# Opening each stage on centred instead of normed tiles at eight layer norms, a new order inside all norms, and the head norms of the second mixer among projections and chunks

## What is computed

```python
# first block, 2 layers: y is an RWKV-7 mixer (layer 0), a gated delta net (layer 1)
    u = x * (1 + sc1) + sh1
    y = mixer(u)
    x = _layer_norm(DEEPNORM_ALPHA * x + (1 + ga1) * y, ln_g[i, 0], ln_b[i, 0])
    u = x * (1 + sc2) + sh2
    gate, up = jnp.split(u @ ffn_w_in[i], 2, axis=-1)
    y = (jax.nn.silu(gate) * up) @ ffn_w_out[i]
    x = _layer_norm(DEEPNORM_ALPHA * x + (1 + ga2) * y, ln_g[i, 1], ln_b[i, 1])
# the delta net's head norms: q and k before the chunks, o behind them
    q = _l2norm(q) * d ** -0.5;  k = _l2norm(k)
    o = _rms_norm(o, norm_g, 1e-6) * jax.nn.silu(z)
# second block, 2 layers: SSD, FoX and MLA branches side by side between two SwiGLU stages
    h = layer_norm(ALPHA * h + 0.5 * swiglu(h, gate1, up1, down1), ln1_g, ln1_b)
    h = layer_norm(ALPHA * h + mix, ln2_g, ln2_b)
    h = layer_norm(ALPHA * h + 0.5 * swiglu(h, gate2, up2, down2), ln3_g, ln3_b)
```

## Time and profile before

| | |
|---|---|
| profiled execution | 2309.86 us, span 2308.0 us |
| median of three executions | 2300.97 us |
| mean granted clock of TensorE | 0.954 |
| TensorE busy | 2120.9 us, 17730 matmuls |
| VectorE busy | 1211.5 us |
| ScalarE busy | 869.0 us |
| GpSimd busy | 707.0 us |
| idle time of TensorE before high-by-high matmuls, put down mostly to ScalarE's normed tile | 63.6 us, 38.0 of them |
| weight splits on GpSimd | 105, 4.67 us each |
| weight splits on VectorE | 132, 2.42 us each |

### The profile page before, as it was taken

How to read it: one execution, slowest core, us unless ns; L and a number is a source line. 1 busy time by engine, 2 the same in 40 slices (tenths; PEclk the granted TensorE clock), 3 DMA queues, 4 the chain that set the end, 5 groups by cost and what they waited for, 6 DMA issues and landing times.

```text
span 2308.0 us, 40812 instructions
## 1 busy us (share of the span) xinstructions
PE 2120.9 (92%) x17730; PEld 1923.8 (83%) x17730; DVE 1211.5 (52%) x2208; ACT 869.0 (38%) x1258; POOL 707.0 (31%) x316
## 2 busy tenths in 40 slices
PE   3989997999889988999999889899999998988997
PEld 3867875889889887898999885699989997857897
DVE  6156444764582446653642656554265428457652
ACT  0442111444353223543433443343343334434543
POOL 0340001314674003126314550131461165304124
PEclk9998998999999989999999998899999999989999
DMA  8564442455434003554445340244434543303552
GB/s 327 226 270 148 149 149 74 146 183 186 157 132 147 2 2 128 186 196 166 162 168 183 128 147 19 91 165 167 181 134 176 175 173 110 128 19 146 184 191 83
DMA packets 49682, 340.44 MB, mean 148 GB/s; under 512 B 6368, under 2 KB 8416, under 8 KB 8672
## 3 DMA queue, kind: packets, MB, share of 16 engines
q1 hardware_dynamic: 49504, 337.84, 40.5%
HBM read 336.77 MB, written 1.05 MB: 146 GB/s over the span
## 4 chain that ended last, share of the span: by engine, by line
PE 80%; DVE 12%; ACT 3%; issue 2%; DMA 2%; POOL 1%; SPq 0%; ACTq 0%; POOLq 0%; DVEq 0%
PE bank L532 80%; DMA ada_ring<-ada 2%; POOL ring_low L2516 1%; DVE arena L1899 1%; DVE arena L1884 1%; ACT high L1471 1%; DVE small L1894 1%; PE bank L538 1%; DVE arena L1927 1%; DVE arena_parts L1922 1%; DVE arena L1914 0%; DVE ZZ L2108 0%; DVE arena L2096 0%; DVE small L2482 0%; DVE small L2371 0%
## 5 line engine op out<-in xcount | busy, mean ns | idle before, releaser
L532 PE MATMUL bank<-arena_parts,high 128*128 128x272 f32 (+2 forms) x4512 | 1028.0, 315 | 63.6 <-ACT arena_parts L1496 38.0
L532 PEld LDWEIGHTS bank<-arena_parts,high 128*128 128x128 f32 x4512 | 751.6, 192 | 114.0 <-issue 52.1
L532 PE MATMUL bank<-arena_parts,ring_low 128*128 128x272 f32 (+2 forms) x2736 | 782.9, 289 | 0.0
L1471 ACT ACTIVATE high<-ring 128x2048 fp32r<-128x2048 f32 x237 | 453.1, 1914 | 681.0 <-PE bank L532 597.1
L2516 POOL TENSOR_TENSOR ring_low<-ring,high 128x2048 fp32r<-128x2048 f32 x105 | 489.7, 4666 | 690.4 <-ACT high L1471 690.3
L532 PEld LDWEIGHTS bank<-arena_parts,ring_low 128*128 128x128 f32 (+1 forms) x2736 | 524.3, 192 | 0.9
L1935 DVE TENSOR_TENSOR ring_low<-ring,high 128x2048 fp32r<-128x2048 f32 x132 | 318.7, 2415 | 185.6 <-ACT high L1471 185.6
L532 PE MATMUL bank<-hidden_high,high 128*128 128x256 f32 (+1 forms) x1056 | 303.2, 287 | 0.0
L532 PE MATMUL bank<-hidden_low,high 128*128 128x256 f32 (+1 forms) x1056 | 301.1, 285 | 0.0
L532 PE MATMUL bank<-hidden_high,ring_low 128*128 128x256 f32 (+1 forms) x1056 | 300.1, 284 | 0.0
L2516 POOL TENSOR_TENSOR hidden_low<-arena,hidden_high 128x256 fp32r<-128x256 f32 (+1 forms) x132 | 105.6, 802 | 586.1 <-DVE hidden_high L1951 585.9
(11 more groups left out here) (330 smaller groups left out, 2272.5 us busy)
## 6 DMA issues: line engine op xcount, KB each, us to landing
ring<-stream SPq DMA_DIRECT2D x269, 1024.0 KB, 4.8
ada_ring<-ada SPq DMA_DIRECT2D x48, 1024.0 KB, 5.6
con<-consts SPq DMA_DIRECT2D x1, 1542.5 KB, 11.5
con<-consts SPq DMA_DIRECT2D x1, 1040.0 KB, 7.1
arena<-xin SPq DMA_DIRECT2D x1, 1024.0 KB, 11.8
out<-arena SPq DMA_DIRECT2D x2, 512.0 KB, 2.9
prob_even<-consts SPq DMA_DIRECT2D x1, 320.0 KB, 11.8
par<-params SPq DMA_DIRECT2D x1, 272.5 KB, 9.7
```

What stands on the lines that cost most here:

```text
L532: ins = nc.tensor.matmul(o, l, r, start=start, stop=stop_, skip_group_check=True)
L1471: act(high[:, q % HIGHS], ring[:, s % RING], ACT.Copy).then_inc(a.sig(high_ready), 1)
```

## The change

1. **Raw openings.** At eight norms (all but 3 and 9) the next stage's first four output tiles are no longer computed from normed tiles but from the centred tiles times the gain, which exist before the variance is known. These raw tiles are split as well: ScalarE writes the high part (`raw_tile`), VectorE the low part (`raw_rest`). Each raw tile carries four further columns with the gain and the bias (high and low), so that the same matmuls, now 260 or 276 columns wide, give the weights' products with gain and bias. `raw_four` issues these matmuls in another order (the eight high ones of a tile, then the four low ones), with the norm's own mean matmuls inside the first tile.
2. **Scaling afterwards.** When the reciprocal of the deviation is there, VectorE mends each of the four banks (`scale_opened`: a reduction of the four columns, one or two multiply-adds, one multiplication). The bias goes into the Silu of the gate, into the product with the up tile, or is added in the bank.
3. **New order in every norm, 3 and 9 too.** All centrings stand behind the variance (three behind the reciprocal), the split of slab 2 moves from GpSimd to VectorE in front of the first normed tile, and ScalarE writes both the high part and the whole input. GpSimd no longer splits between the normed tiles; in a mixer stage slab 3 is split there by GpSimd once the last low part is made.
4. **Base tiles later.** `residual_base` leaves the norm: in a feed-forward stage with a raw opening it stands behind f=1, in mixers behind the third convolution.
5. **A shift for the last tile.** `early_mean` gains a third matmul, half_mean into bank 6, from which the last tile's centring reads.
6. **Head norms of the delta net.** The sums and spreadings of q and k move among the last eight projection tiles. The squares of the output are made per chunk by ScalarE and summed by TensorE inside the chunk loop (`output_sums`), with one small result per group of four heads.

The core of the diff:

```diff
 def low_by_vector_engine(q):
 
     n = max(i for i in range(len(STAGES)) if STAGE_AT[i] <= q)
-    return STAGES[n] == "ffn" and HIGHS <= q - STAGE_AT[n] < HIGHS + FT
+    at = q - STAGE_AT[n]
+    return at == HIGHS - 1 or STAGES[n] == "ffn" and HIGHS <= at < HIGHS + FT
...
                 eng.wait_ge(*freed(4))
                 mm(bank[4][:, 0:T], cm("mean"), x_sums(0, T), True, False)
                 mm(bank[4][:, 0:T], cm("mean"), x_sums(1, T), False, False)
+                mm(bank[6][:, 0:T], cm("half_mean"), x_sums(0, T), True, True, hold=True).then_inc(full["vector"][6], 1)
...
+            def raw_four(n, tiles, T, signals):
+
+                for b in range(4):
+                    eng.wait_ge(*freed(b))
+                eng.wait_ge(square_added, pe.nth(square_added, 6))
+                eng.wait_ge(raw_high_ready, pe.nth(raw_high_ready, 1))
+                eng.wait_ge(raw_low_ready, pe.nth(raw_low_ready, 1))
+                for k in range(DT):
+                    eng.wait_ge(raw_high_ready, pe.nth(raw_high_ready))
+                    eng.wait_ge(raw_low_ready, pe.nth(raw_low_ready))
+                    blocks = [split_block((*tile, k)) for tile in tiles]
+                    both, low = raw_both(n, k, T), raw_low(n, k, T)
+                    if k == DT - 1:
+                        for b, (w_high, w_low) in enumerate(blocks):
+                            m = mm(bank[b][:, 0:T], w_high, low, False, False, hold=b == 3)
+                        m.then_inc(opened, 1)
+                    for b, (w_high, w_low) in enumerate(blocks):
+                        if k == 0 and b == 2:
+                            mean_sum(T)
+                        mm(bank[b][:, 0:T + 4], w_high, both, k == 0, False)
+                        m = mm(bank[b][:, 0:T + 4], w_low, both, False, k == DT - 1, hold=k == DT - 1)
+                        if k == DT - 1:
+                            m.then_inc(signals[b], 1)
+                    if k == 0:
+                        square_sum(T)
+                    if k < DT - 1:
+                        for b, (w_high, w_low) in enumerate(blocks):
+                            m = mm(bank[b][:, 0:T], w_high, low, False, False, hold=b == 3)
+                        m.then_inc(opened, 1)
+
+            def normal_tile():
+
+                eng.wait_ge(input_high_ready, pe.nth(input_high_ready))
+                eng.wait_ge(input_low, pe.nth(input_low))
+
...
-            left(-(-at[0] // BLOCKS))
-
+            project_by_parts("gdn", "gdn_in", 0, 2, SEQ, [0, 1], "scalar", n0=24)
             eng.wait_ge(a2p, pe.nth(a2p))
             token_sums(8, 4)
             token_sums(3, 5)
+            project_by_parts("gdn", "gdn_in", 0, 2, SEQ, [2, 3], "scalar", n0=26)
             eng.wait_ge(v2p, pe.nth(v2p))
-            spread_scale(0, B4)
+            spread_scale(0, [4, 5, 6, 7])
+            project_by_parts("gdn", "gdn_in", 0, 2, SEQ, [0, 1], "scalar", n0=28)
             eng.wait_ge(v2p, pe.nth(v2p))
-            spread_scale(1, B4)
+            spread_scale(1, [4, 5, 6, 7])
+            project_by_parts("gdn", "gdn_in", 0, 2, SEQ, [2, 3], "scalar", n0=30)
+            left(-(-at[0] // BLOCKS))
 
             eng.wait_ge(a2p, pe.nth(a2p))
...
+            def output_sums(p, c):
+
+                eng.wait_ge(head_squares, pe.nth(head_squares, 2))
+                if c == 0:
+                    eng.wait_ge(*freed(3))
+                for hb in range(4):
+                    m = mm(bank[3][:, 2 * hb + c:2 * hb + c + 1], tl(US, 4 * p + hb, SEQ, META)[:, P * c:P * c + P], one[:, :],
+                           True, True, hold=c and hb == 3)
+                if c:
+                    m.then_inc(closing(3, "vector"), 1)
...
+            def raw_tile(n, j, T):
+                act(raw_high(n, j, T), tl(9, j, T), ACT.Copy, scale=lnc[:, n, 0, j:j + 1]).then_inc(a.sig(raw_high_ready), 1)
...
+            def norm_out(n, T):
+                raw = n in OPENED_RAW
+                weights_high(STAGE_AT[n] + 2)
+                if raw:
+                    done = a.nth(opened, DT) - DT
                 for j in range(DT):
                     eng.wait_ge(normed, a.nth(normed))
-                    if n < len(STAGES):
-                        act(input_high(STAGES[n], j, T), tl(9, j, T), ACT.Identity, bias=lnc[:, n, 1, j:j + 1],
+                    if raw:
+                        eng.wait_ge(opened, done + max(min(j + 2, DT - 1), j + 1))
+                    for to, signal in ((input_high(STAGES[n], j, T), input_high_ready), (tl(US, j, T, xview(T)), whole_ready)):
+                        act(to, tl(9, j, T), ACT.Identity, bias=lnc[:, n, 1, j:j + 1],
                             scale=lnc[:, n, 0, j:j + 1]).then_inc(a.sig(signal), 1)
...
+            def raw_rest(n, js, T):
...
+                for j in js:
+                    if j == 0:
+                        eng.wait_ge(raw_high_ready, v.nth(raw_high_ready))
+                        for i, (to, gains, part) in enumerate(raw_columns(n, T, 1)):
+                            nv.tensor_tensor(to, gains, part.bitcast(F32), ALU.subtract).then_inc(v.sig(raw_low_ready if i else vstep), 1)
+                    eng.wait_ge(raw_high_ready, v.nth(raw_high_ready))
+                    nv.scalar_tensor_tensor(out=raw_low(n, j, T), in0=tl(9, j, T), scalar=lnc[:, n, 0, j:j + 1],
+                                            in1=raw_high(n, j, T).bitcast(F32), op0=ALU.mult,
+                                            op1=ALU.subtract).then_inc(v.sig(raw_low_ready), 1)
...
+            def norm(n, T, order):
+                raw = n in OPENED_RAW
+                raw_rest(n, order[1][0], T)
                 eng.wait_ge(full_for_vector[4], v.nth(full_for_vector[4]))
-                nv.tensor_tensor(small[:, 0, 0:T], bank[4][:, 0:T], small[:, 1, 0:T], ALU.subtract).then_inc(v.sig(shift_ready), 1)
-
+                nv.tensor_tensor(small[:, 0, 0:T], small[:, 1, 0:T], bank[4][:, 0:T], ALU.subtract).then_inc(v.sig(shift_ready), 1)
+                raw_rest(n, order[1][1], T)
+                eng.wait_ge(full_for_vector[5], v.nth(full_for_vector[5]))
+                eng.wait_ge(shift_squared, v.nth(shift_squared))
+                nv.scalar_tensor_tensor(out=small[:, 1, 0:T], in0=bank[5][:, 0:T], scalar=EPS_LN, in1=small[:, 2, 0:T],
+                                        op0=ALU.add, op1=ALU.subtract).then_inc(v.sig(var_ready), 1)
+                raw_rest(n, order[1][2], T)
...
                 centers = [center(0)]
-                eng.wait_ge(full_for_vector[5], v.nth(full_for_vector[5]))
...
                 nv.reciprocal(small[:, 2, 0:T], small[:, 1, 0:T]).then_inc(v.sig(vstep), 1)
+                centers += [center(1), center(2), center(3)]
+                if n < len(STAGES):
+                    weights_low(STAGE_AT[n] + 2)
+
+                def normed_pair(q):
+                    for j in (2 * q, 2 * q + 1):
+                        eng.wait_ge(*centers[3])
+                        nv.tensor_tensor(tl(9, j, T), tl(XAS, j, T, xview(T)), small[:, 2, 0:T], ALU.mult).then_inc(v.sig(normed), 1)
+
+                normed_pair(0)
+                normed_pair(1)
+                for q in range(4):
+                    if n < len(STAGES):
+                        for j in (2 * q, 2 * q + 1):
+                            eng.wait_ge(input_high_ready, v.nth(input_high_ready))
+                            eng.wait_ge(whole_ready, v.nth(whole_ready))
+                            nv.tensor_tensor(input_rest(j, T), tl(US, j, T, xview(T)), input_high(STAGES[n], j, T).bitcast(F32),
+                                             ALU.subtract).then_inc(v.sig(input_low), 1)
+                    if q < 2:
+                        normed_pair(q + 2)
...
+            def scale_opened(b, T, signal, to_bias):
+
+                both = bank[b][:, T:T + 4].rearrange("p (a e) -> p a e", e=2)
+                nv.tensor_reduce(opening_cols[:, b], both, AX_X, ALU.add).then_inc(v.sig(vstep), 1)
...
+                product = bank[b][:, 0:T]
+                for i in range(1 if to_bias else 2):
+                    nv.scalar_tensor_tensor(out=product, in0=small[:, i, 0:T], scalar=opening_cols[:, b, i:i + 1], in1=product,
+                                            op0=ALU.mult, op1=ALU.add).then_inc(v.sig(vstep), 1)
+                    eng.wait_ge(*v.last)
+                nv.tensor_tensor(product, product, small[:, 2, 0:T], ALU.mult).then_inc(v.sig(signal), 1)
...
+                raw = n in OPENED_RAW
+                if not raw:
+                    residual_base(n, T if n != 3 else SEQ)
+                    weights_low(q0 + HIGHS)
+                full_gate = v.nth(gate_full, FT) - FT
                 for f in range(FT):
+                    up = bank[2 * (f % 3) + 1][:, 0:T]
+                    if f < 2 and raw:
+                        eng.wait_ge(gate_full, full_gate + f + 1)
+                        scale_opened(2 * f, T, gate_scaled, True)
```

(31 more changed lines are left out.)

302 lines of the change are left out of this document (166 added, 136 removed).

## The result

| | before | after |
|---|---|---|
| median, six executions each | 2300.48 us | 2322.57 us (2313.47 to 2324.27) |
| ratio | | 1.0085, 95% interval 1.0068 to 1.0103 |
| profiled execution: span | 2308.0 us | 2322.1 us |
| mean granted clock | 0.954 | 0.953 |

The kernel is 0.85% slower. The forecast was 2320 us, slower, in a range of 2292 to 2344. The two profiled spans differ by 14.1 us, the medians by 22.1: the profiled execution of before lay 9.4 us over its median, that of after 1.6. Where 4.5 of these 8 us are is shown further down.

What follows compares the result with a forecast made beforehand. The prediction took TensorE, busy 92% of the span, as the bound. Its terms, -5.7+6.2+12.1+3.2+3.65+4.4-3-2.5+3, gave +21.3 us on the profiled 2309.86; scaled to the median 2322, stated as 2320 us, range 2292 to 2344.

Steps and rivals of the forecast that it cites:

- step (3): Feed-forward stages: VectorE's longer chain spends the won 9 us in stalls at f=2, f=3 and f=5; sum -5.7 us.
- Steps (1) to (3): Feed-forward openings: TensorE ends norm 0's opening at 426.6 rather than 434.6, VectorE's chain gets longer; sum -5.7 us.
- Step (4): Norm 1, before the delta net: late low halves and scaled convolutions put the seventh convolution at 666.1; +6.2 us.
- Step (5): Norms 4 and 7: scaled convolutions delay the fifth's Silu, for which TensorE's sixth tile waits; sum +12.1 us.
- step (11): TensorE's clock may fall to 1.2 GHz at f=2, before f=3 and in mixers; 0 to +8 us, taken as +3.
- Step (6): Norms 1, 4, 6, 7: GpSimd's splits hold VectorE's raw low halves, 0.8 us each; +3.2 us.
- rival (c): GpSimd's split of the second opening slab holds raw low halves, 3 us in each of four norms; 2336 us, chance 0.15.
- Steps (7), (8): Norms 3 and 9 get the new order without raw openings, +3.65 us; each norm gets a third mean matmul, +4.4 us.
- Steps (9), (10): Delta net: head norms among the last eight projection tiles, -3 us; output sums inside the chunk loop, -2.5 us.
- (a): Rival at the openings: VectorE's way to the split for f=3 is shorter than priced; 2286 us, chance 0.20.
- (b): Rival: clock and GpSimd terms nil, head norms give all, scaling costs a third less; 2306 us, chance 0.20.
- (d): Rival: raw openings wait 1 to 2 us for weights at norms 1, 4, 6, 7; forecast's time, joint chance 0.45.

Runs made afterwards that it cites:

- e2: Kernel before with raw openings at norms 1, 4, 7 alone (in front of the mixers), all else as before: 2315.81 us, ratio 1.0066.
- e8: Kernel before with only the head norms among the projection tiles and the output sums in the chunk loop: 2302.87 us, ratio 1.0009.
- e1: Raw openings at norms 0, 2, 5, 6, 8 alone (in front of feed-forward stages), other norms and head norms as before: 2300.25 us, ratio 1.0001.
- e3: Changed kernel with slab 3 split earlier, by VectorE behind the fourth normed tile, in the five raw feed-forward openings: 2306.93 us.
- e9: Kernel before with the new order of the norm at norms 3 and 9 alone, no raw opening: 2307.38 us, ratio 1.0025.
- e4: Changed kernel without scaling the opened banks before the convolutions of the delta net and both mixers (computation left out): 2301.70 us.
- e5: e1 with the order of e3 (slab 3 split by VectorE behind the fourth normed tile): 2291.88 us, ratio 0.9968 to the kernel before.
- e7: e6 with the whole input of tiles 5 and 7 written by VectorE instead of ScalarE: 2280.10 us, ratio 0.9914 to the kernel before.
- e6: e5 without the third mean matmul and with base tiles behind f=4 and f=5 instead of f=1: 2281.80 us, ratio 0.9922 to the kernel before.

## Why the prediction was right, and where it wasn't

**Time and direction: right; the sum behind it partly by errors that cancel.** It was 21.3 us on the profiled execution; the profiled pair shows 14.1, the medians 22.1. The four parts run alone add up: 1 + 0.0001 + 0.0066 + 0.0009 + 0.0025 = 1.0101, beside 1.0085 (1.0068 to 1.0103) for all. The steps as measured below come to -2.8 + 3.3 + 9.1 + 0 + 3.3 + 4.4 + 0 + 1 = 18 us, inside the interval of 16 to 24. The forecast is close since what it had too low (the feed-forward openings by 2.9, the head norms by 5.5) and too high (delta net 2.9, three-branch mixers 3.0, GpSimd 3.2, clock 2) nearly cancel: that part is luck.

**The profiled execution of before has four costly boundaries.** The same code gives f=6 earlier in e2 and e8: 0.8, 2.0 to 2.3, 0.8 and 0.8 us at norms 2, 5, 6 and 8, 4.5 us in all. At norm 5 of before:

```profile
1503.43 5.69 POOL L2516 TENSOR_TENSOR ring_low<-ring,high 128x2048 fp32r<-128x2048 f32 x1 [25.93 <-ACT high L1471]
...
1505.13 6.15 DVE L1935 TENSOR_TENSOR ring_low<-ring,high 128x2048 fp32r<-128x2048 f32 x1 [0.42 <-ACT high L1471]
...
1509.27 0.36 PE L532 MATMUL bank<-arena_parts,high 128*128 128x272 f32 x1 [1.82 <-POOL ring_low L2516]
```

GpSimd's split took 5.69 us. VectorE's, which lasts 2.28 us alone, began beside it and ended 2.15 us behind its end: it was held, and not slowed down. All four norms show this pair. TensorE waited 1.82 us for GpSimd's split; in e8 there is no such wait. What the other 3 of the 8 us are isn't shown; the mixers' scatter covers them. So the profiled pair understates the loss, and step (3) took its gain from a bad boundary.

**Steps (1) to (3), the feed-forward openings.** The mechanism is right to 0.4 us: first normed tile forecast 424.3, measured 424.36; last low half 433.3 and 433.32; f=3 439.5 and 439.64 (all with a projection that ended 0.37 later); f=6 at +43.4 and +43.08. The wait in front of f=3, forecast 3 us, is 0.42 to 2.56, by how much of it the lower clock in f=2 fills; f=3 starts at the same place either way (+25.27 at norms 0 and 2, with waits of 0.42 and 1.47). The size was -5.7 us; against undisturbed boundaries it is 0 for the three norms of 256 columns and -1.4 for each of 272, -2.8. With 2.2 us of mean matmuls e1 is a wash. VectorE's and ScalarE's chain gave back the 7.7 us by which TensorE's opening ends sooner (+12.92, e8 +20.64).

**Step (4), the delta net: +6.2 forecast, +3.3 measured.** The term that failed is "the decay rows 14.0 as now". Lines of before, with GpSimd's splits, and what answers to them after:

```profile
638.61 9.16 POOL L2516 TENSOR_TENSOR ring_low<-ring,high 128x2048 fp32r<-128x2048 f32 x2 [3.15 <-ACT high L1471]
...
645.87 2.04 DVE L2204 TENSOR_SCALAR arena<-arena 8x256 f32<-8x256 f32 x1
...
649.31 4.60 POOL L2516 TENSOR_TENSOR ring_low<-ring,high 128x2048 fp32r<-128x2048 f32 x1 [1.54 <-ACT high L1471]
649.73 4.47 DVE L2208 TENSOR_TENSOR arena<-arena 8x256 f32<-8x256 f32 x1
654.23 0.41 DVE L2210 TENSOR_TENSOR arena<-arena 8x256 f32<-8x256 f32 x1
```

```profile
652.98 0.27 DVE L2386 TENSOR_SCALAR arena<-arena 8x256 f32<-8x256 f32 x1
...
653.44 4.60 POOL L2709 TENSOR_TENSOR ring_low<-ring,high 128x2048 fp32r<-128x2048 f32 x1 [0.87 <-ACT high L1590]
655.06 3.27 DVE L2390 TENSOR_TENSOR arena<-arena 8x256 f32<-8x256 f32 x1
...
664.03 0.45 DVE L2411 TENSOR_SCALAR XX<-bank,par 128x256 f32<-128x256 f32 x1
...
666.53 0.58 PE L576 MATMUL bank<-arena_parts,high 128*128 128x256 f32 x1 [6.31 <-ACT arena L1776]
```

In before both instructions stand beside a split and end 0.1 and 0.3 us behind its end, at 647.8 and 653.9. After the change the first falls between two splits and takes 0.27 us. The second still stands beside one, and ends 0.3 us behind that one's end too (658.04), but it began later within it: 3.27 us. The next instruction of its kind, beside no split, takes 0.41. So the decay rows last 11.1 us and not 14.0: the two were held for 1.8 and 1.2 us less, by where GpSimd's splits happen to fall. In e2 and e3, also raw here, it is 11.05 and 11.04 us, in the kernels with the old opening 14.0. The Trainium skill ("GPSIMD Engine Reference", section 8, Key points) has VectorE and GpSimd share SBUF access for instructions of two-port modes or with two SBUF inputs; both rows of before agree. I used it for a cost of the change and missed the same cost inside a price of before.

**Step (5), the three-branch mixers: +12.1 forecast, +9.1 to +10 measured** (40.80-36.23 and 40.78-36.23, or less the 35.38 of before's profile). Place and releaser were right:

```profile
1304.45 0.44 DVE L2009 SCALAR_TENSOR_TENSOR arena<-bank,arena 128x272 f32<-128x272 f32 x1 [3.91 <-PE bank L576]
...
1324.07 1.05 DVE L2084 SCALAR_TENSOR_TENSOR bank<-small,opening_cols,bank 128x272 f32<-128x272 f32 x2
...
1343.04 1.57 DVE L2414 SCALAR_TENSOR_TENSOR arena<-bank,par,arena 128x271 f32<-128x271 f32 x3
...
1344.64 0.52 ACT L1853 ACTIVATE arena<-arena,par 128x272 f32<-128x272 f32 x1 [1.09 <-DVE arena L2414]
...
1345.21 0.59 PE L576 MATMUL bank<-arena_parts,high 128*128 128x272 f32 x1 [8.51 <-ACT arena L1853]
```

The first five convolutions ended 1.5 us earlier than I had (Silu at +40.2, forecast +41.7). Behind it TensorE runs at a granted 0.65 until 1352, some of step (11). Over the two stages as a whole the changed kernel has 387.6 us, of which 0.9 are third mean matmuls, and the seven profiles with the old opening 376.3 on average without such matmuls: +10.4, so about 1 us comes behind the tile.

**Step (6), GpSimd beside the raw low halves: +3.2 forecast, near 0.** The raw low halves are held, as rival (c) said, and for as long. At norm 4 of the changed kernel:

```profile
1295.65 9.36 POOL L2709 TENSOR_TENSOR ring_low<-ring,high 128x2048 fp32r<-128x2048 f32 x2 [3.91 <-ACT high L1590]
...
1296.86 3.68 DVE L1975 SCALAR_TENSOR_TENSOR arena_parts<-arena,lnc,arena_parts 128x272 fp32r<-128x272 f32 x1
```

This one takes 3.68 us instead of 0.49, until 0.3 us behind the end of the first of the two splits; at norms 6 and 7 it is the same and at norm 1 it is 4.17 us. But it stands before the last projection tile, where VectorE then still waits 3.91 us for TensorE (1304.45 above): it costs nothing. Behind that tile only norm 1 has a held one, 1.08 us instead of 0.48. From the residual of the last tile to the reciprocal it is 4.71 us there and 4.35 at norm 0, with no split beside it; norms 4 and 7 have 4.50 us, as norm 5 without a split. So (c) had the mechanism right and the place wrong.

**Steps (7), (8): right.** f=6 behind norm 3 at +47.71, before +44.91: 2.8 us (3.5 in e9); from norm 9's last residual to the end 14.42 us, before 13.90: 0.5; each third mean matmul 0.44 (from norm 0 to norm 1 it is 196.74 us, before 196.26, of which f=6 has 0.04).

**Steps (9), (10), the head norms: -5.5 forecast, nothing shown.** The spreads do run at the full clock, 3.73 us for 32 as forecast, but the sums take 10.39 at a granted 0.68 (forecast 7.0, before 8.98 at 0.78), and the stretch from the seventh tile to the transposes is 84.84 us, before 84.82. From the transposes to the output scale it is 107.5 us in the profiles of the changed kernel and e8 and about 106.5 in most profiles of the old form; but 101.4 in e3 and e4 and 102.0 in e5, which has the old form. Where it is over 106 us the two passes have 10.2 to 13.7 us each at half clock, in e3 and e4 6.8 each. The clock's part, up to 6 us between two profiles of the same code, is larger than what the change does there.

**Step (11), the clock.** It fell at f=2 as forecast (not at norm 6), but the split of slab 3 covered it; the +3 belongs to the mixers only, and there it is about 1.

**Rivals.** (a) named the way to win: a shorter way to the split. It didn't come with this change, but e3 makes it, with 2.4 us per norm. (b), a wash at 2306, is outside the measured interval (2316 to 2324). (c) had VectorE held, but where it had time to spare. (d) didn't occur: no gap in any of the eight openings is over 0.1 us.

**Still open:** why TensorE's clock falls in one execution and not in another for the same code, in the chunk loop and in the stretch before norm 0; and why e5 keeps 8 of 12 us.

## What to carry to other kernels

When an engine is idle at a boundary, price the chain that ends the idle time, and the one behind it: an opening that starts 6.7 us earlier was worth nothing where VectorE's work behind it grew by as much, and cost 4.6 us where 7 us of mending stood in front of a shared bank. The order inside that chain was worth more than the idea: moving one 2.3 us split into a wait gave 2.4 us per norm, and e7, raw only where it pays, is 0.9% faster than before. Take a boundary's price from several executions, or from the same code at several places; one profile overstated it by 2 us. And look whether an instruction in such a price was held by another engine: its length then says when the other ended, and moves with it.

## What the runs showed of the hardware

- In f=2 at norm 0 TensorE was busy for 2.85 of 4.45 us in bursts 0.98 us apart when its clock fell to 1.2 GHz; in e3 it was busy for 3.84 of 6.50, after one pause of 1.1 us, and the clock stayed. Less idle time isn't always a higher clock. Nor is it always the same for the same code: in f=2 the clock fell at four of the five raw norms of the changed kernel, at all five of e1, and at one of the twenty of e3, e5, e6 and e7.
- The same code in the chunk loop takes 101.4 to 107.5 us, at a granted 0.95 or 0.89.
- Beside a split of GpSimd, some VectorE instructions don't run slower but are held until the split ends: of those shown, a split of 128x2048 (2.28 us alone) ended 2.15 us behind it, a tensor_tensor of 8x256 (0.41) and a raw low half (0.49) 0.3 us behind it, whenever they began.
